# Triangular inverse in one bank: each square made, copied and turned whole, in place of two halves in two banks

## The chip, the cores and the metric

One core of one Trainium2 chip. The time is the device time of the program in microseconds (us); lower is better.

## The reference

One transformer block: four token mixers side by side (gated linear attention, RWKV, Mamba and gated DeltaNet) over 1280 tokens (256 of context, 1024 in a grid), each run forwards and backwards with 4 heads of 64, then a mixture of 64 experts. The change touches two of the mixers. DeltaNet solves, for every chunk of 64 tokens, head and direction, a unit lower triangular system of 64 x 64:

```python
a_kk = jnp.einsum('bnhid,bnhjd->bnhij', kb, k) * jnp.exp(jnp.where(strict, seg, -jnp.inf))
sol = lax.linalg.triangular_solve(a_kk, rhs, left_side=True, lower=True, unit_diagonal=True)
```

RWKV is a step-by-step recurrence there, and the kernel brings it into the same chunked form with the same kind of inverse. In both, a state of 64 x 64 per head and direction then goes from chunk to chunk.

## The kernel before, in words

The program runs in stages, one after the other; every stage has a queue of instructions for each engine, in a written order, tied together by semaphores. `deltanet` (from L1395) and `rwkv` (from L2047) each end in a scan over 10 **pairs** of chunks. One pair holds 8 matrices of 64 x 64 (two directions, two chunks, two heads) for each of two halves of the partitions, so one array of 128 x 512 holds all 16 of a pair. A pair's matrices are inverted while the pair before goes through the state.

`Solve` (L1231) makes the inverse. With N the negated strict part, cut into levels by GpSimd (L1831 to L1833: blocks of 16, the level to 32 and the level to 64), it squares the blocks of 16 three times and sums up Y: square, y2, fourth, y4, eighth, y8; then t32, y32 and t64, y64 join the blocks. For a square TensorE needs both N (copied out of PSUM by ScalarE, L1322) and its transpose M (turned from N by VectorE, L1346; the record of it stands under L1330, the helper). In `scalar` and `vector` these are two operations of 128 x 256 each, for half 0 and half 1; `squared` (L1266) puts half 0 into bank 0 and half 1 into bank 1, and signals after each. The products y2, y4, y8 and the t's and y's go through `product` (L1258), whole, into bank 2 or bank 1; VectorE adds them to Y (L1334), ScalarE copies t32 and t64 (L1325). The eighth isn't turned. `PE_AT`, `ACT_AT` and `DVE_AT` number the signals.

`weave` (L1967) lays out each engine's queue by one list for each mixer; the number is the pair to which an entry belongs, 0 the one being inverted, 1 the next, -1 the one that goes through the state:

```python
DELTA_ORDER = (("square", 0), ("against 0", -1), ("y2", 0), ("solve 0", -1), ("decay 0", -1), ("fourth", 0),
               ("rows", 1), ("result 0", -1), ("y4", 0), ("grams", 1), ("eighth", 0), ("query rows", 1), ("y8", 0),
               ("against 1", -1), ("t32", 0), ("solve 1", -1), ("decay 1", -1), ("y32", 0), ("result 1", -1), ("turn", 1),
               ("t64", 0), ("query grams", 1), ("y64", 0))
```

In DeltaNet "against" is TensorE L1754 and L1762, then VectorE L1915 and L1924 (the right-hand side); "solve" TensorE L1775 and ScalarE L1869; "result" TensorE L1794 and L1802 and VectorE L1936 to L1943 (L1942 where an output is added to an earlier one); "rows" TensorE L1703, VectorE L1887, ScalarE L1859; "grams" TensorE L1717, VectorE L1894, and GpSimd's L1821 and the level masks; "query rows" VectorE L1902, after GpSimd's causal terms (L1821 again); "query grams" TensorE L1729. The first two pairs have no query part. On GpSimd the masks stand ahead of the causal terms. RWKV's list (`WIDE_ORDER`, L1986) weaves in its own grams (TensorE L2329, VectorE L2528), state products and exponentials (ScalarE L2477 to L2479) the same way.

Of the kernel before, what the change touches and what calls it, by code (L numbers as in the profile page):

```python
# [19 lines left out]
NH, HD = 4, 64  # L20
# [82 lines left out]
def each(ap, n):  # L103

    return ap.unsqueeze(1).to_broadcast([ap.shape[0], n, ap.shape[1]])
# [1088 lines left out]
def half(n):  # L1194

    return slice(HD * n, HD * n + HD)
# [34 lines left out]
class Solve:  # L1231

    NPE, NACT, NDVE = 13, 8, 11
    PE_AT = {"square0": 1, "square1": 2, "y2": 3, "fourth0": 4, "fourth1": 5, "y4": 6, "eighth0": 7, "eighth1": 8,
             "y8": 9, "t32": 10, "y32": 11, "t64": 12, "y64": 13}
    ACT_AT = {"square0": 1, "square1": 2, "fourth0": 3, "fourth1": 4, "eighth0": 5, "eighth1": 6, "t32": 7, "t64": 8}
    DVE_AT = {"square0_turned": 1, "square1_turned": 2, "y2": 3, "fourth0_turned": 4, "fourth1_turned": 5, "y4": 6,
              "y8": 7, "y8_turned": 8, "y32": 9, "y32_turned": 10, "y64": 11}  # L1240

    def __init__(self, nc, sem, cr, consts, banks):
        self.nc, self.c, self.banks = nc, consts, banks
# [5 lines left out]
    def pe_done(self, eng, p, what):  # L1249
        eng.wait_ge(self.pe_s, p * self.NPE + self.PE_AT[what])  # L1250

    def act_done(self, eng, p, what):
        eng.wait_ge(self.act_s, p * self.NACT + self.ACT_AT[what])

    def dve_done(self, eng, p, what):
        eng.wait_ge(self.dve_s, p * self.NDVE + self.DVE_AT[what])

# [5 lines left out]
                                             start=True, stop=True)  # L1263
        last.then_inc(self.pe_s, 1)

    def squared(self, n, lhsT, rhs):  # L1266
        for x in range(4 * n, 4 * n + 4):
            for a in range(2):
                r = half(a)
                last = self.nc.tensor.matmul(self.banks[n][r, (x - 4 * n) * HD:(x - 4 * n + 1) * HD], lhsT[r, x],  # L1270
                                             rhs[r, x], start=True, stop=True)
        last.then_inc(self.pe_s, 1)

    def tensor(self, pe, what, p):
        N0, N32, N64, Y = (b[:, p % 2] for b in (self.N0, self.N32, self.N64, self.Y))
        if what == "square":
            pe.wait_ge(self.turned, p + 1)
            for n in range(2):
                self.squared(n, self.M, N0)
        elif what == "y2":  # L1280
            self.act_done(pe, p, "square1")
            pe.wait_ge(self.begun, p + 1)
            if p >= 1:
                self.dve_done(pe, p - 1, "y64")
            self.product(2, self.N, Y)
        elif what == "fourth":
            for n in range(2):
                self.dve_done(pe, p, f"square{n}_turned")
                self.squared(n, self.M, self.N)
        elif what == "y4":  # L1290
            self.act_done(pe, p, "fourth1")
            self.dve_done(pe, p, "y2")
            self.product(2, self.N, Y)
        elif what == "eighth":
            for n in range(2):
                self.dve_done(pe, p, f"fourth{n}_turned")
                self.squared(n, self.M, self.N)
        elif what == "y8":
            self.act_done(pe, p, "eighth1")
            self.dve_done(pe, p, "y4")  # L1300
            self.product(2, self.N, Y)
        elif what == "t32":
            self.dve_done(pe, p, "y8")
            self.product(1, N32, Y)
        elif what == "y32":
            self.act_done(pe, p, "t32")
            self.dve_done(pe, p, "y8_turned")
            self.product(2, self.X, self.T)
        elif what == "t64":
            self.dve_done(pe, p, "y32")  # L1310
            self.product(1, N64, Y)
        elif what == "y64":
            self.act_done(pe, p, "t64")
            self.dve_done(pe, p, "y32_turned")
            self.product(2, self.X, self.T)

    def scalar(self, act, what, p):
        b = [bank[:, :].rearrange("p (x j) -> p x j", x=8) for bank in self.banks]
        if what in ("square", "fourth", "eighth"):
            for n in range(2):  # L1320
                self.pe_done(act, p, f"{what}{n}")
                self.nc.scalar.copy(self.N[:, 4 * n:4 * n + 4], b[n][:, 0:4]).then_inc(self.act_s, 1)  # L1322
        elif what in ("t32", "t64"):
            self.pe_done(act, p, what)
            self.nc.scalar.copy(self.T, b[1]).then_inc(self.act_s, 1)  # L1325

    def vector(self, dve, what, p):
        Y = self.Y[:, p % 2]
        flat = lambda b: b.rearrange("p x j -> p (x j)")
        turn = lambda dst, src: self.nc.vector.transpose(flat(dst), flat(src))  # L1330

        def add(made):
            self.pe_done(dve, p, made)
            self.nc.vector.tensor_tensor(Y, Y, self.banks[2].rearrange("p (x j) -> p x j", x=8),  # L1334
                                         ALU.add).then_inc(self.dve_s, 1)

        if what == "turn":
            turn(self.M, self.N0[:, p % 2]).then_inc(self.turned, 1)
            dve.wait_ge(self.turned, p + 1)
            self.nc.vector.tensor_tensor(Y, self.M, each(self.c.ident, 8), ALU.add).then_inc(self.begun, 1)  # L1340
        elif what in ("square", "fourth"):
            if what == "square":
                dve.wait_ge(self.begun, p + 1)
            for n in range(2):
                self.act_done(dve, p, f"{what}{n}")
                turn(self.M[:, 4 * n:4 * n + 4], self.N[:, 4 * n:4 * n + 4]).then_inc(self.dve_s, 1)  # L1346
        elif what == "y2":
            add("y2")
        elif what == "y4":
            self.dve_done(dve, p, "y2")  # L1350
            add("y4")
        elif what == "y8":
            self.dve_done(dve, p, "y4")
            add("y8")
        elif what == "t32":
            self.dve_done(dve, p, "y8")
            turn(self.X, Y).then_inc(self.dve_s, 1)
        elif what == "y32":
            add("y32")
            self.dve_done(dve, p, "y32")  # L1360
            turn(self.X, Y).then_inc(self.dve_s, 1)
        elif what == "y64":
            add("y64")
# [2299 lines left out]
```

## Time and profile before

| | |
|---|---|
| median of 3 runs | 2801.02 us (2797.8 to 2801.89) |
| the profiled execution | 2796.13 us |
| its span on the core | 2794.5 us |
| TensorE matmul busy | 2504.4 us (90%) |
| VectorE busy | 1538.3 us (55%) |
| ScalarE busy | 974.8 us (35%) |
| GpSimd busy | 838.9 us (30%) |
| L1262, products, 4480 matmul records | 172.8 us |
| granted TensorE clock, mean | 0.952 |

How to read it: the span is one execution as the profiler saw it, and an engine's share of it is an average over stages that have nothing in common. A matmul in 32-bit floats leaves two records; a product or a square of a pair is 16 matmuls, so 32 records. "PE" is TensorE's matmuls, "PEld" its weight loads, DVE is VectorE, ACT ScalarE, POOL GpSimd. "x2" in a row of the order of time means that instructions of one line were merged; the time is then from the first start to the last end. The bracket gives the idle time of the engine before it and who ended it.

### The profile page before, as it was taken

To read this page: it belongs to the slowest core of one execution; us is meant where nothing else is said; L and a number is where in the kernel's file an instruction comes from. 1 tells how busy PE (TensorE), PEld (TensorE's weight loads), DVE (VectorE), ACT (ScalarE), POOL (GpSimd) and SP (SyncE) were. 2 spreads that over 40 slices of the span, in tenths; PEclk is the share of its full clock that TensorE was granted. 3 is DMA by queue.
4 is the path that set the end of the run, shared out by engine and by line. 5 is a ranking of instruction groups with operands and counts; after the bars stand their busy time and mean duration, and the time that the engine had idled before them with its cause. 6 is when DMAs were issued, how large, how long until landed. Compare 5 with 4: busy or idle time off the path is not lost. (4 is left out here: it accounts for less than half of the span.)

```text
span 2794.5 us, 72353 instructions
## 1 busy us (share of the span) xinstructions
PE 2504.4 (90%) x27195; PEld 1379.4 (49%) x27196; DVE 1538.3 (55%) x2685; ACT 974.8 (35%) x1707; POOL 838.9 (30%) x654
## 2 busy tenths in 40 slices
PE   5999899889788869899979797899999999999956
PEld 2448358645578735599834352333333333333322
DVE  3106365844556622476544585566666666666538
ACT  2613115412222202333211113455555555555411
POOL 1000000000244200111100003566666666666565
PEclk9999999899989979999989998999999999999978
DMA  6001402120000020000032207898998899772177
GB/s 243 17 0 47 139 16 91 50 76 1 2 3 4 3 73 1 1 4 5 4 137 95 76 38 309 325 358 348 354 354 319 328 344 357 268 272 89 69 309 315
DMA packets 109099, 408.11 MB, mean 146 GB/s; under 512 B 21001, under 2 KB 37083, under 8 KB 83932
## 3 DMA queue, kind: packets, MB, share of 16 engines
q1 hardware_dynamic: 76636, 287.71, 27.8%
q0 software_dynamic: 20736, 75.51, 6.9%
q10 hardware_dynamic: 11520, 41.95, 3.8%
q8 instruction: 153, 2.51, 0.4%
q14 instruction: 54, 0.44, 0.0%
HBM read 346.40 MB, written 58.72 MB: 145 GB/s over the span
## 5 line engine op out<-in xcount | busy, mean ns | idle before, releaser
L3266 PE MATMUL bank<-arena 128*32 x1280 | 567.6, 596 | 10.5 <-SPq L68 8.1
L3268 PE MATMUL bank<-arena 128*32 128x512 f32 x3840 | 568.6, 596 | 0.0
L3227 POOL COPY arena<-arena 128x2048 f32 x240 | 448.7, 1903 | 330.0 <-PE bank L3300 328.5
L3266 PEld LDWEIGHTS bank<-arena 128*32 128x32 f32 x1280 | 134.7, 110 | 358.4 <-issue 349.3
L3297 PE MATMUL bank<-arena 128*32 x640 | 289.9, 596 | 5.5 <-POOL arena L3227 5.5
L3300 PE MATMUL bank<-arena 128*32 128x512 f32 x1920 | 290.9, 596 | 0.0
L3421 DVE COPY arena<-arena 128x2048 f32 x80 | 139.3, 1741 | 201.6 <-PE bank L3268 183.2
L3358 ACT COPY arena<-arena 128x2048 f32 x80 | 152.0, 1900 | 197.2 <-PE bank L3268 137.8
L1262 PE MATMUL bank<-arena 64*64 64x64 f32 x4480 | 172.8, 226 | 41.9 <-DVE arena L1334 35.1
L3217 POOL DMA_INDIRECT arena<-normed_rows,arena x80 | 165.1, 2064 | 148.8 <-DVE arena L3405 136.9
L1262 PEld LDWEIGHTS bank<-arena 64*64 64x64 f32 x4480 | 157.9, 141 | 47.0 <-DVE arena L1334 37.1
L3297 PEld LDWEIGHTS bank<-arena 128*32 128x32 f32 x640 | 70.4, 110 | 198.4 <-issue 197.9
L3364 ACT COPY arena<-arena 128x2048 f32 x80 | 152.1, 1901 | 0.0
L3268 PEld LDWEIGHTS bank<-arena 128*32 128x32 f32 x3840 | 150.5, 110 | 0.0
L3399 DVE TENSOR_SCALAR arena<-bank,arena 128x128 f32<-128x128 f32 x320 | 109.3, 403 | 40.5 <-PE bank L3251 40.5
L1500 PE MATMUL bank<-arena 128*128 128x512 f32 (+1 forms) x320 | 129.6, 565 | 0.3 <-PE bank L1500 0.3
L517 PE MATMUL bank<-arena 128*128 128x512 f32 (+1 forms) x320 | 127.3, 552 | 0.0
L2462 POOL TENSOR_TENSOR arena<-arena 128x512 f32<-128x512 f32 x10 | 12.9, 1286 | 368.6 <-DVE arena L2528 255.0
L3333 ACT ACTIVATE arena<-bank,arena 128x128 f32<-128x128 f32 x320 | 121.1, 466 | 3.4 <-PE bank L3251 3.4
L351 POOL MEMSET arena<- 128x256 f32 x2 | 0.6, 312 | 394.4 <-POOLq L442 227.5
L1381 DVE SCALAR_TENSOR_TENSOR arena<-arena 128x945 f32<-128x945 f32 (+2 forms) x96 | 113.8, 1220 | 1.7
L2747 PE MATMUL bank<-arena 128*128 128x512 f32 x256 | 111.9, 595 | 0.0
(555 smaller groups left out, 4566.8 us busy)
## 6 DMA issues: line engine op xcount, KB each, us to landing
arena<-in_exp_w_gate_dram SPq DMA_DIRECT2D x64, 1024.0 KB
arena<-in_exp_w_up_dram SPq DMA_DIRECT2D x64, 1024.0 KB
arena<-in_exp_w_down_dram SPq DMA_DIRECT2D x64, 1024.0 KB, 9.3
expert_rows<-arena ACTq DMA_DIRECT2D x80, 512.0 KB
arena<-in_w_mod_dram SPq DMA_DIRECT2D x32, 512.0 KB, 9.1
arena<-in_x_dram SPq DMA_DIRECT2D x16, 512.0 KB, 6.3
arena<-in_w_mod_dram SPq DMA_DIRECT2D x8, 1024.0 KB, 17.8
arena<-in_w_in_dram SPq DMA_DIRECT2D x12, 384.0 KB, 5.9
```

Source lines behind the costliest of these rows:

```text
L517: last = nc.tensor.matmul(k.ps[p % 4][:, 0:width], k.hT[:, c, t * P:(t + 1) * P], W[g][:, c, ws], start=(c == 0), stop=(c == KC - 1))
L1262: last = self.nc.tensor.matmul(self.banks[bank][r, x * HD:(x + 1) * HD], lhsT[r, x], rhs[r, x], start=True, stop=True)
L1500: last = nc.tensor.matmul(k.ps[p % 4][:, 0:w], W[m // 3 % 2][:, c, (m % 3) * P:(m % 3 + 1) * P], k.hT[:, c, a:a + w], start=(c == 0), stop ...
L3217: nc.gpsimd.indirect_dma_start(out=G[:, b.q], out_offset=None, in_=xn_dram, in_offset=bass.IndirectOffsetOnAxis(ap=ID[:, b.q], axis=0)).th ...
L3227: last = nc.gpsimd.tensor_copy(down_copy(u), down_of(slots[u]))
L3266: nc.tensor.matmul(out(SUB - 1), XTT[:, b.q, c, rows(SUB - 1)], W[:, :, c], start=first, stop=end)
L3268: last = nc.tensor.matmul(out(u), XTT[:, b.q, c, rows(u)], WC[:, u, :, c], start=first, stop=end)
L3297: nc.tensor.matmul(ps[6 + half][rows(SUB - 1), :], HT[:, b.q, f, rows(SUB - 1)], W[:, f, c], start=(f == 0), stop=(f == 1))
L3300: last = nc.tensor.matmul(ps[6 + half][rows(u), :], HT[:, b.q, f, rows(u)], WDC[:, u, f, c], start=(f == 0), stop=(f == 1))
L3358: nc.scalar.copy(copy_of(2, LOW), part_of(slot, LOW)).then_inc(lo_a, 1)
L3364: nc.scalar.copy(copy_of(2, HIGH), part_of(slot, HIGH)).then_inc(hi_a, 1)
L3421: nc.vector.tensor_copy(copy_of(0, LOW), part_of(slots[0], LOW))
```

## The change

All three squares use `product` into bank 0. ScalarE makes one copy of 128 x 512 in place of two of 128 x 256, VectorE one transposition of 128 x 512 in place of two; TensorE waits once, for the whole, where it waited once for each half. The signals are renumbered. `squared` is gone. The order of the stages is the same, and `Solve` serves both mixers.

```diff
--- before.py
+++ after.py
@@ -1232,12 +1232,11 @@
 
 
 
-    NPE, NACT, NDVE = 13, 8, 11
-    PE_AT = {"square0": 1, "square1": 2, "y2": 3, "fourth0": 4, "fourth1": 5, "y4": 6, "eighth0": 7, "eighth1": 8,
-             "y8": 9, "t32": 10, "y32": 11, "t64": 12, "y64": 13}
-    ACT_AT = {"square0": 1, "square1": 2, "fourth0": 3, "fourth1": 4, "eighth0": 5, "eighth1": 6, "t32": 7, "t64": 8}
-    DVE_AT = {"square0_turned": 1, "square1_turned": 2, "y2": 3, "fourth0_turned": 4, "fourth1_turned": 5, "y4": 6,
-              "y8": 7, "y8_turned": 8, "y32": 9, "y32_turned": 10, "y64": 11}
+    NPE, NACT, NDVE = 10, 5, 9
+    PE_AT = {"square": 1, "y2": 2, "fourth": 3, "y4": 4, "eighth": 5, "y8": 6, "t32": 7, "y32": 8, "t64": 9, "y64": 10}
+    ACT_AT = {"square": 1, "fourth": 2, "eighth": 3, "t32": 4, "t64": 5}
+    DVE_AT = {"square_turned": 1, "y2": 2, "fourth_turned": 3, "y4": 4, "y8": 5, "y8_turned": 6, "y32": 7,
+              "y32_turned": 8, "y64": 9}
 
     def __init__(self, nc, sem, cr, consts, banks):
         self.nc, self.c, self.banks = nc, consts, banks
@@ -1263,40 +1262,29 @@
                                              start=True, stop=True)
         last.then_inc(self.pe_s, 1)
 
-    def squared(self, n, lhsT, rhs):
-        for x in range(4 * n, 4 * n + 4):
-            for a in range(2):
-                r = half(a)
-                last = self.nc.tensor.matmul(self.banks[n][r, (x - 4 * n) * HD:(x - 4 * n + 1) * HD], lhsT[r, x],
-                                             rhs[r, x], start=True, stop=True)
-        last.then_inc(self.pe_s, 1)
-
     def tensor(self, pe, what, p):
         N0, N32, N64, Y = (b[:, p % 2] for b in (self.N0, self.N32, self.N64, self.Y))
         if what == "square":
             pe.wait_ge(self.turned, p + 1)
-            for n in range(2):
-                self.squared(n, self.M, N0)
+            self.product(0, self.M, N0)
         elif what == "y2":
-            self.act_done(pe, p, "square1")
+            self.act_done(pe, p, "square")
             pe.wait_ge(self.begun, p + 1)
             if p >= 1:
                 self.dve_done(pe, p - 1, "y64")
             self.product(2, self.N, Y)
         elif what == "fourth":
-            for n in range(2):
-                self.dve_done(pe, p, f"square{n}_turned")
-                self.squared(n, self.M, self.N)
+            self.dve_done(pe, p, "square_turned")
+            self.product(0, self.M, self.N)
         elif what == "y4":
-            self.act_done(pe, p, "fourth1")
+            self.act_done(pe, p, "fourth")
             self.dve_done(pe, p, "y2")
             self.product(2, self.N, Y)
         elif what == "eighth":
-            for n in range(2):
-                self.dve_done(pe, p, f"fourth{n}_turned")
-                self.squared(n, self.M, self.N)
+            self.dve_done(pe, p, "fourth_turned")
+            self.product(0, self.M, self.N)
         elif what == "y8":
-            self.act_done(pe, p, "eighth1")
+            self.act_done(pe, p, "eighth")
             self.dve_done(pe, p, "y4")
             self.product(2, self.N, Y)
         elif what == "t32":
@@ -1317,9 +1305,8 @@
     def scalar(self, act, what, p):
         b = [bank[:, :].rearrange("p (x j) -> p x j", x=8) for bank in self.banks]
         if what in ("square", "fourth", "eighth"):
-            for n in range(2):
-                self.pe_done(act, p, f"{what}{n}")
-                self.nc.scalar.copy(self.N[:, 4 * n:4 * n + 4], b[n][:, 0:4]).then_inc(self.act_s, 1)
+            self.pe_done(act, p, what)
+            self.nc.scalar.copy(self.N, b[0]).then_inc(self.act_s, 1)
         elif what in ("t32", "t64"):
             self.pe_done(act, p, what)
             self.nc.scalar.copy(self.T, b[1]).then_inc(self.act_s, 1)
@@ -1341,9 +1328,8 @@
         elif what in ("square", "fourth"):
             if what == "square":
                 dve.wait_ge(self.begun, p + 1)
-            for n in range(2):
-                self.act_done(dve, p, f"{what}{n}")
-                turn(self.M[:, 4 * n:4 * n + 4], self.N[:, 4 * n:4 * n + 4]).then_inc(self.dve_s, 1)
+            self.act_done(dve, p, what)
+            turn(self.M, self.N).then_inc(self.dve_s, 1)
         elif what == "y2":
             add("y2")
         elif what == "y4":
```

## Rows read from the trace of the kernel before

**Rows 1.** Stretch: length, then busy us (x instructions) of PE, PEld, DVE, ACT, POOL; clock

```profile
736.00:982.00 246.00, 194.90 (x5800) 188.97 (x5795) 147.65 (x287) 55.11 (x120) 93.91 (x180) 0.91 0.01 3
1157.00:1391.00 234.00, 220.70 (x7232) 217.67 (x7232) 148.27 (x256) 76.82 (x201) 39.16 (x30) 0.99 0.02 4
```

**Rows 2.** The waits in DeltaNet's scan: who waited for whom, us, times, longest

```profile
DVE arena L1902 <- POOL arena L1821: 43.0, 8, 5.4
```

**Rows 3.** Order of time, DeltaNet's pair 3: start, us, engine, line, shape, [idle before]

```profile
809.48 1.10 PE L1270 MATMUL bank<-arena 64*64 64x64 f32 x32
...
810.16 0.84 ACT L1322 COPY arena<-bank 128x256 f32<-128x256 f32 x2 [1.75 <-PE bank L1270]
...
810.63 0.84 DVE L1330 STREAM_TRANSPOSE arena<-arena 128x256 f32<-128x256 f32 x2 [0.25 <-ACT arena L1322]
...
811.56 0.42 DVE L1915 TENSOR_TENSOR arena<-bank,arena 128x256 f32<-128x256 f32 x1
...
812.02 0.42 DVE L1924 TENSOR_TENSOR arena<-arena 128x256 f32<-128x256 f32 x1
...
812.59 0.68 PE L1775 MATMUL bank<-arena 64*64 64x64 f32 x16
...
818.03 0.69 DVE L1894 SCALAR_TENSOR_TENSOR arena<-bank,arena 128x512 f32<-128x512 f32 x1 [0.20 <-PE bank L1717]
```

**Rows 4.** Order of time, DeltaNet's pair 9: whole copies and turns

```profile
963.71 0.59 ACT L1325 COPY arena<-bank 128x512 f32<-128x512 f32 x1 [3.25 <-PE bank L1262]
...
964.34 1.15 PE L1262 MATMUL bank<-arena 64*64 64x64 f32 x32
...
966.33 0.71 DVE L1330 STREAM_TRANSPOSE arena<-arena 128x512 f32<-128x512 f32 x1
...
966.97 0.38 DVE L1936 TENSOR_TENSOR arena<-arena,bank 128x256 f32<-128x256 f32 x1
```

**Rows 5.** Order of time, DeltaNet's pairs 1 (first two rows) and 7

```profile
762.20 1.10 PE L1270 MATMUL bank<-arena 64*64 64x64 f32 x32
...
764.12 0.39 DVE L1915 TENSOR_TENSOR arena<-bank,arena 128x256 f32<-128x256 f32 x1
...
912.74 0.69 DVE L1334 TENSOR_TENSOR arena<-arena,bank 128x512 f32<-128x512 f32 x1
```

**Rows 6.** Order of time, pair 3 again: from the fourth to y8

```profile
813.08 1.13 PE L1270 MATMUL bank<-arena 64*64 64x64 f32 x32
...
815.23 0.69 DVE L1887 TENSOR_TENSOR arena<-bank,arena 128x512 f32<-128x512 f32 x1
...
816.11 0.42 DVE L1936 TENSOR_TENSOR arena<-arena,bank 128x256 f32<-128x256 f32 x1 [0.19 <-PE bank L1802]
...
817.14 0.69 DVE L1334 TENSOR_TENSOR arena<-arena,bank 128x512 f32<-128x512 f32 x1 [0.28 <-PE bank L1262]
...
817.74 1.13 PE L1270 MATMUL bank<-arena 64*64 64x64 f32 x32
...
819.61 1.13 PE L1262 MATMUL bank<-arena 64*64 64x64 f32 x32
```

**Rows 7.** Order of time, DeltaNet's pair 0: the eighth and y8

```profile
752.04 1.10 PE L1270 MATMUL bank<-arena 64*64 64x64 f32 x32
...
753.61 1.15 PE L1262 MATMUL bank<-arena 64*64 64x64 f32 x32 [0.47 <-ACT arena L1322]
```

**Rows 8.** Order of time, a pair of RWKV's scan

```profile
1209.35 1.15 PE L1270 MATMUL bank<-arena 64*64 64x64 f32 x32
...
1211.21 1.15 PE L1262 MATMUL bank<-arena 64*64 64x64 f32 x32
...
1215.73 0.69 DVE L2528 TENSOR_TENSOR arena<-bank,arena 128x512 f32<-128x512 f32 x1 [0.68 <-PE bank L2329]
```

**Rows 9.** Order of time: TensorE's first product after the wait, pairs 2 and 3

```profile
801.14 1.97 PE L1262 MATMUL bank<-arena 64*64 64x64 f32 x32 [4.24 <-DVE arena L1334]
...
825.43 1.15 PE L1262 MATMUL bank<-arena 64*64 64x64 f32 x32 [3.76 <-DVE arena L1334]
```

## The prediction

> **What bounds the kernel now.** The lines that change run in two stretches only, so I first took the busy time of each engine in them: DeltaNet's scan, 736 to 982 us, and RWKV's, 1157 to 1391 us [rows 1]. In RWKV's, TensorE is busy for 220.7 of 234 us: it is bound by what TensorE issues. In DeltaNet's it is busy for 194.9 of 246 us, so something in a chain sets the pace there. The waits name it: VectorE stands still before line 1902, query rows, 43.0 us over 8 pairs for GpSimd's causal terms (L1821) [rows 2]. GpSimd makes them only behind the three level masks, and those need the negated gram of L1894. So in a DeltaNet pair (ten in 246 us; pair 0 is the first) everything ahead of L1894 counts, and what comes after it and before L1902 has 5 us of cover.
>
> Then I followed one pair, pair 3, in order of time [rows 3]. The square's 32 matmul records start at 809.48 and end at 810.58. ScalarE copies half 0 from 810.16, while TensorE still makes half 1; VectorE turns the halves from 810.63 to 811.47. Next on VectorE's queue is L1915 at 811.56, which subtracts the state's part from the right-hand side, and TensorE's L1775 (solve 0, 812.59) waits for its result. From L1775 on TensorE has next to no idle time up to L1717, the key grams, and L1894 follows them at 818.03. So what delays L1915 delays the pair.
>
> **What a whole square costs in its place.** The products are the same: 32 records, the same order, 1.10 us. 120 half copies become 60 whole ones, 80 half transpositions 40, and the signals and waits between halves go. Not shown before is the copy of a whole square, but the same copy out of bank 1 is [rows 4]: 0.59 us, TensorE's next product 0.04 us after its end. A whole transposition is there too: 0.71 us, and the next VectorE work starts 0.64 us after its start. From TensorE's end to ScalarE's start I take 0.05 us (half of the records of 809.48, and so half 0, are through at about 810.1, and its copy starts at 810.16), from the end of a copy to VectorE about 0.10 (810.16 + 0.37 to 810.63).
>
> *First square, pairs 3 to 9.* The product ends at 810.58, copy 810.63 to 811.22, turned from 811.32, L1915 at 811.96 in place of 811.56: +0.40 us. The y2 product sits behind the state's matmuls and isn't late. Nothing between L1915 and L1894 gives it back: 7 x 0.40 = 2.8 us.
>
> *First square, pairs 1 and 2.* The state's product is shorter there (no query part), and L1915 already starts at 764.12, with the square ended at 763.30 [rows 5]. By the same steps it comes at 764.68: 2 x 0.56 = 1.1 us.
>
> *Fourth.* Product from 813.08 to 814.21; copy 814.26 to 814.85; turned from 814.95; the next, L1887, at 815.59 in place of 815.23, so 0.36 us more [rows 6]. L1936 had 0.19 us of idle time before it and the y4 sum 0.28: both are used up, and L1894 isn't later. In the pairs whose output is added to an earlier one, the y4 sum (912.74) shows no idle time [rows 5], and 0.36 - 0.19, say 0.15, gets through. Of those, pairs 7 and 8 still have an L1894 behind them: 0.3 us.
>
> *Eighth.* Product 817.74 to 818.87, copy to 819.51, y8 product at 819.55 or a little later against 819.61 now, which stands behind the query grams [rows 6]. Nothing; and its sum waits for L1902 anyhow. If that cover went, it would cost what the next case does.
>
> *Ends of the scans.* Where no other work stands between square and product, the wait shows in full: in DeltaNet's first pair the eighth ends at 753.14 and y8 starts at 753.61 [rows 7]; after, 753.14 + 0.05 + 0.59 + 0.04 = 753.82, so +0.21. There are five such places (first square and eighth of DeltaNet's first pair, the eighth of its last, and the eighths of RWKV's first and last): 1.05 us.
>
> *RWKV's pairs.* TensorE is busy through. The fourth ends at 1210.50 [rows 8]; a whole copy ends at 1211.14; the y4 product (1211.21, weights 0.05 ahead) is late by 0.02 us at most. The first square's copy stands there behind the exponentials on ScalarE's queue, so the whole isn't later. VectorE turns 0.1 to 0.2 us later, and its idle 0.68 us before the second L2528 takes that up. 8 x 0.02 = 0.2 us.
>
> Sum: 2.8 + 1.1 + 0.3 + 1.05 + 0.2 = **+5.5 us**. The profiled execution took 2796.13 us (span 2794.5 and 1.6 around it); with +5.5 it is 2801.6. It was the quickest shown: the median of the three runs is 2801.02, 4.9 above. Against that median I forecast **2806.5 us**. A measurement of this kernel can tell about 0.2%, or 5.6 us, from no change, so the forecast stands on that line.
>
> Bounds of the unseen costs: the 0.40 and 0.56 rest on a copy of 0.59, seen 40 times, and on hand-over times of 0.04 to 0.15. With 0.05 us either way on each of nine pairs the sum moves by 0.5; with the fourths let through in all ten pairs by 0.36 it grows by 3.3; with no first square on the path only 1.5 is left.
>
> **TensorE's clock.** After the wait before L1902, TensorE comes back at either level: after 4.24 us idle, in pair 2, the next product took 1.97 us, the 1.2 GHz level; after 3.76 us idle, in pair 3, it took 1.15, the 2.4 GHz level [rows 9]. So 0.82 us hangs on where in that idle time a fall lands. In the profile that product is quick in the six pairs from 3 to 8. Pairs that grow by 0.4 us meet the falls elsewhere. I put it at nothing against the median, whose runs differ by 4.1 us; against the profile up to 6 x 0.82 = 4.9 more, or, where a pair escapes a slow product that it pays now, 0.82 less each, some 2 in all. The Trainium skill (TensorE: Matmul & The Clock Gate, "The HAM clock gate") says that the idle state is the throttled one and that activity releases it, so it would have products after every such pause slow. The row at 825.43 disagrees; by the rule alone that product would be slow in every pair, before and after alike, and the change would get nothing from the clock.
>
> **Rivals.** *A, slower by clearly more:* the drift against the clock's falls puts the product after the wait (t32, L1304) at the low level in five of those six pairs too. It decides once a fall reaches back over that product's start. 5.5 + 5 x 0.82 = 9.6 us: 2810.6. For it: pair 2 shows it. Against: the runs of before sample such positions too.
>
> *B, not slower:* the halves' overlap buys nothing, because L1915 isn't what TensorE really waits for before L1775, or because one long operation hands over quicker than two. The place is the gap of 0.25 us before L1775's weights; it decides if that gap belongs to TensorE's own issue, as its row says. Then only the 1.05, the 0.2 and some of the 0.3 are left: +1.5, or 2802.5. Against: L1775 starts 0.15 us after L1924's end in pair after pair, and L1924 cannot start before L1915 ends.
>
> *C, faster:* two copies of 0.37 are 0.15 us more than one of 0.59, and two half turns take 0.84 us from end to end against 0.71. If ScalarE's or VectorE's occupancy were what each square waits for, 60 x 0.15 would be 9 us less: 2792. Against: ScalarE is idle 1.75 us before the copy [rows 3]. The Trainium skill (VectorE: DVE Perf Modes, "The TRN2 errata", on a fixed extra latency per instruction) argues for this case: fewer and larger operations pay it once. The rows agree on the size; they disagree that it is on the path.
>
> *D, no effect:* the schedule is hidden behind GpSimd altogether, so the time is 2801. That needs L1902's wait to start from something other than L1894.
>
> **How the numbers follow.** Forecast (4 to 7 us) 0.50, split evenly about the line of 5.6 us; A 0.22; B and D together 0.22; C 0.06. Slower by over 0.2%: 0.25 + 0.22 = 0.47. Within 0.2%: 0.25 + 0.22 = 0.47. Faster: 0.06. The range reaches from B to a little over A, 2801.5 to 2811.5, and leaves out D, C, and the worst of the clock.
>
> **What would show it.** Right: in DeltaNet's pairs 3 to 9 the square's matmuls end, one ScalarE copy of 0.59 starts 0.05 us later, and L1915 starts 1.38 us after that end, where it was 0.98; L1775 keeps its 0.15 behind L1924; VectorE's wait before query rows stays at 43 us in all; DeltaNet's scan grows from 246 to some 251 us, and RWKV's by no more than 1. Wrong: L1915 as near to the square as before, DeltaNet's scan as long as before, or a gap on TensorE ahead of y4 in RWKV's pairs. Then the handing over between the engines was misread.

## The result, and the profile after: slower by 9 us, where 5.5 were forecast

Over 12 runs of each kernel the changed one takes 2808.85 us and the one before 2799.81 (medians); the ratio is 1.0032, with a 95% interval of 1.0021 to 1.0044, or +9.0 us (5.9 to 12.3). The forecast was +5.5 and 2806.5 us, with a range of 2801.5 to 2811.5. The sign and the range held, and the size was low. The profiled execution took 2806.82 us with a span of 2805.1.

L1262 is now L1261 (all products, the squares too); the copy of a square is L1309, of t32 and t64 L1312, the turn L1317, the sums L1321. The scans' own lines are 14 lower (L1915 is L1901, L1924 is L1910, L1775 is L1761, L1894 is L1880, L1902 is L1888). One reading of the prediction is put right here, since the text below uses it: L1915 (now L1901) only multiplies the state's product by its decay factors; the subtraction is L1924 (now L1910), right behind it. The chain is the same. The two scans answer to [rows 1]: DeltaNet's from ScalarE's first activation in it (L1841) to VectorE's first output work behind it, then the same 234 us of RWKV's.

```profile
735.50:986.70 251.20, 196.44 (x5824) 191.00 (x5824) 141.57 (x268) 51.24 (x90) 94.72 (x182) 0.91 0.01 3
...
1157.00:1391.00 234.00, 220.24 (x6995) 214.78 (x6995) 138.79 (x229) 72.37 (x168) 39.51 (x30) 0.97 0.02 4
```

VectorE and ScalarE are busy for less, as rival C wanted, and the scan is longer all the same. Measured in every trace from the start of one line to the start of another (DeltaNet: L1855 to L2033 of before; RWKV: the first L2514 to the first L2655), DeltaNet's scan went from 246.67 to 251.13 us (+4.46; forecast +4.9) and RWKV's from 241.11 to 244.67 (+3.56; forecast +0.6). The other 2.6 us of the two spans' 10.6 lie outside the scans, in code that did not change.

The waits in DeltaNet's scan, who waited for whom, us, times, longest; this answers to [rows 2]:

```profile
DVE arena L1888 <- POOL arena L1807: 43.0, 8, 5.4
```

Unchanged to the tenth: everything that L1894 (now L1880) loses, the pair loses. Pair 3 in order of time, against [rows 3] and [rows 6]:

```profile
812.19 2.03 PE L1261 MATMUL bank<-arena 64*64 64x64 f32 x64
...
814.27 0.58 ACT L1309 COPY arena<-bank 128x512 f32<-128x512 f32 x1 [2.21 <-PE bank L1261]
...
814.96 0.71 DVE L1317 STREAM_TRANSPOSE arena<-arena 128x512 f32<-128x512 f32 x1 [0.93 <-ACT arena L1309]
...
815.59 0.39 DVE L1901 TENSOR_TENSOR arena<-bank,arena 128x256 f32<-128x256 f32 x1
816.01 0.43 DVE L1910 TENSOR_TENSOR arena<-arena 128x256 f32<-128x256 f32 x1
...
816.59 0.68 PE L1761 MATMUL bank<-arena 64*64 64x64 f32 x16 [0.50 <-DVE arena L1910]
...
821.14 0.69 DVE L1321 TENSOR_TENSOR arena<-arena,bank 128x512 f32<-128x512 f32 x1 [0.26 <-PE bank L1261]
...
822.03 0.69 DVE L1880 SCALAR_TENSOR_TENSOR arena<-bank,arena 128x512 f32<-128x512 f32 x1 [0.20 <-PE bank L1703]
```

The first row holds an earlier product and the square together; they end at 812.19 + 2.03 = 814.22. The copy starts 0.05 later and takes 0.58, and L1901 starts at 815.59, 1.37 us after the square's end, where 1.38 was forecast and 0.98 measured before. L1761 starts 0.15 after L1910's end, and now shows 0.50 us of idle time. The y4 sum has kept 0.26 us of its idle time, so the whole fourth passes nothing on.

The distances between successive L1894s, each ending in the pair named (us), show where DeltaNet's 4.46 came from; "rest" is from the last of them to the end of the scan:

| ends in pair | 0 | 1 | 2 | 3 | 4 | 5 | 6 | 7 | 8 | rest |
|---|---|---|---|---|---|---|---|---|---|---|
| before | 13.32 | 17.78 | 23.64 | 24.30 | 24.07 | 23.70 | 23.75 | 23.82 | 23.85 | 44.51 |
| after | 15.04 | 18.55 | 24.30 | 24.65 | 24.11 | 24.05 | 24.12 | 24.16 | 24.17 | 44.03 |
| forecast change | 0.21 | 0.77 | 0.56 | 0.40 | 0.40 | 0.40 | 0.40 | 0.55 | 0.55 | 0.61 |
| measured change | 1.72 | 0.77 | 0.66 | 0.35 | 0.04 | 0.35 | 0.37 | 0.34 | 0.32 | -0.48 |

Pairs 1 to 3 and 5 to 8 are near the forecast. **Pair 0** is the mis-sized one: 1.5 us too little was allowed. Its start after the change, and behind it the same stretch before:

```profile
744.76 1.98 PE L1261 MATMUL bank<-arena 64*64 64x64 f32 x32 [7.12 <-DVE arena L1317]
...
746.78 0.58 ACT L1309 COPY arena<-bank 128x512 f32<-128x512 f32 x1 [7.40 <-PE bank L1261]
...
747.42 3.68 PE L1261 MATMUL bank<-arena 64*64 64x64 f32 x64 [0.69 <-ACT arena L1309]
...
750.89 1.66 PE L1689 MATMUL bank<-arena 64*64 64x64 f32 x32
```

```profile
744.27 1.97 PE L1270 MATMUL bank<-arena 64*64 64x64 f32 x32 [7.12 <-DVE arena L1330]
...
746.71 1.76 PE L1262 MATMUL bank<-arena 64*64 64x64 f32 x32 [0.47 <-ACT arena L1322]
...
748.30 1.10 PE L1270 MATMUL bank<-arena 64*64 64x64 f32 x32
...
749.24 1.10 PE L1703 MATMUL bank<-arena 64*64 64x64 f32 x32
```

The idle time before y2 grew by 0.22 us, as the forecast said of such places. But before, TensorE was back at 2.4 GHz within y2 (1.76 us) and made the fourth in 1.10; after, y2 and the fourth both run at 1.2 GHz (3.68 us for the two, 1.0 more than before), and the rise comes within the key rows behind them (L1689, 1.66 us for 1.10). That is 0.2 + 1.0 + 0.6 us, and pair 0 grew by 1.72. The same 11.5 us of each trace, after and then before; the granted clock is the third number from the end (0.55 and 0.70):

```profile
741.00:752.50 11.50, 7.06 (x132) 6.87 (x134) 3.66 (x5) 1.17 (x2) 7.68 (x15) 0.55 0.01 1
```

```profile
741.00:752.50 11.50, 7.76 (x208) 7.58 (x210) 5.59 (x10) 2.12 (x5) 7.20 (x15) 0.70 0.01 3
```

### The profile page after: what moved, and what is told of

Its sections match the earlier page's. It is cut to its first block and busy times, and to the rows that moved or that the text cites. A ratio compares the mean times of both kernels' runs of the same rounds, so it can differ in the third digit from the quotient of the medians.

```text
span 2805.1 us, 72253 instructions
## 1 busy us (share of the span) xinstructions
PE 2511.4 (90%) x27195; PEld 1387.2 (49%) x27196; DVE 1526.8 (54%) x2645; ACT 965.6 (34%) x1647; POOL 838.4 (30%) x654
## 5 line engine op out<-in xcount | busy, mean ns | idle before, releaser
L1261 PE MATMUL bank<-arena 64*64 64x64 f32 x6400 | 241.6, 226 | 52.6 <-DVE arena L1321 34.9
L1261 PEld LDWEIGHTS bank<-arena 64*64 64x64 f32 x6400 | 222.0, 142 | 58.5 <-DVE arena L1321 37.0
L1807 POOL TENSOR_TENSOR arena<-arena 128x128 f32<-128x128 f32 x72 | 27.8, 415 | 283.5 <-SPq L1677 283.5
```

Source lines behind the costliest of these rows:

```text
L1261: last = self.nc.tensor.matmul(self.banks[bank][r, x * HD:(x + 1) * HD], lhsT[r, x], rhs[r, x], start=True, stop=True)
```

## Experiments

Differences in us are the ratio times the median of before in the same group of runs; they can be off the difference of the two medians by a few tenths to 3 us. The first group, e1 to e4, has a median of 2795.80 us for before.

The first group asks whether the loss is DeltaNet's or RWKV's, and the first square's or the others'. An argument names the powers that are made whole; the rest stay halves:

```
-    inv = Solve(nc, sem, cr, H, k.ps[0:3])
+    inv = Solve(nc, sem, cr, H, k.ps[0:3], whole)
e1: whole = all three in DeltaNet, none in RWKV
e2: whole = none in DeltaNet, all three in RWKV
e3: whole = ("square",) in both
e4: whole = ("fourth", "eighth") in both
```

**e1.** 

> Whole squares in DeltaNet's scan, halves in RWKV's. Theory (the chain from the first square over VectorE's turn and L1915 to solve 0): DeltaNet's scan, from ScalarE's L1855 to VectorE's L2033, grows from 246.7 us to about 251 us as in the changed kernel (251.1), RWKV's stays as before; the whole kernel 4 to 5 us slower. Rival (RWKV's scan carries the rest of the 9 us): then this kernel shows only half of the loss, and the next one the other half. Rival (clock): DeltaNet's scan is off from 251 by more than 1 us, and RWKV's first two pairs (28.6 us before, 32.1 after) differ although their code is that of before.

Measured: 2805.49 us against 2795.80, ratio 1.0037 (1.0024 to 1.0050), +10.3 us. DeltaNet's scan 253.46 us, RWKV's 241.09. So nearly all of the loss is DeltaNet's, but it is twice the 4 to 5 us expected; the last distance is 26.48 in place of some 24.1, to which e9 comes back. RWKV's first two pairs take 28.46 us here, with halves.

**e2.** 

> Whole squares in RWKV's scan, halves in DeltaNet's. Theory: DeltaNet's scan 246.7 us; RWKV's pairs 2 to 9 as long as before, its first two pairs at most 0.5 us longer at the same clock; the whole kernel 0 to 1 us slower. Rival (RWKV's scan loses 3.5 us by the change itself): its first two pairs take 32 us here too, with TensorE at its full clock, and the kernel is 3 to 5 us slower. Rival (clock): the first two pairs are longer only where their matmuls run at the low clock.

Measured: 2800.33 us, ratio 1.0014 (1.0000 to 1.0028), +3.9 us (0 to 7.8), where 0 to 1 was expected; the interval holds both. DeltaNet's scan 246.90, RWKV's 242.52, its first two pairs 29.03 us where the changed kernel's profile has 32.10. So those 3.5 us of the changed kernel's profile do not come with whole squares. Whole squares in RWKV cost some tenths to 1.4 us in the traces.

**e3.** 

> Only the first square of each pair whole, the fourth and the eighth in halves, in both mixers. Theory: VectorE's L1915 comes 0.40 us later in DeltaNet's pairs 3 to 9 and 0.56 in pairs 1 and 2; the scan takes 250.5 to 251 us, nearly all of the loss. Rival (the loss is spread over the three squares, some 0.15 each): 248 us.

Measured: 2804.20 us, ratio 1.0023 (1.0013 to 1.0033), +6.4 us (3.6 to 9.2); DeltaNet's scan 250.95, its distances 15.06, 18.33, 24.40, 24.66, 24.16, 24.08, 24.03, 24.10, 24.18. Within 0.25 us these are the changed kernel's own: the first square carries the whole loss that DeltaNet's trace shows.

**e4.** 

> The fourth and the eighth whole, the first square in halves, in both mixers. Theory: DeltaNet's scan grows by 0.4 (eighths of pairs 0 and 9) plus 0.3 (fourths of pairs 7 and 8): 247.4 us; L1915 as before; the kernel within 0.1% of before. Rival (loss spread over the squares): 249.5 us and some 3 to 5 us slower.

Measured: 2795.42 us, ratio 1.0008 (0.9998 to 1.0018); DeltaNet's scan 247.52, first distance 13.24, then 23.56 to 23.82 from pair 3 to 7 and 24.53 in pair 8. In pair 2 it is 25.44, with a VectorE operation of 2.82 us in it (e9). Fourth and eighth are hidden, as the forecast said. That the scan is near the expected 247.4 is luck: the long operation adds some 2 us, and pair 3 and the rest (43.69) are shorter than before by 1.6. In pair 8 the extra 0.7 us are a product of 1.29 for 1.10 and a stop of TensorE amid the 16 matmuls of L1824 (L1802 of before), for which no row names a cause.

The second group, e5 to e8, has a median of 2801.14 us for before. It asks whether it is really L1915's lateness, and what whole squares cost where GpSimd is no longer waited for.

**e5.** An idle VectorE product of 128x448 ahead of L1915, with halves, for the same delay from another cause:

```
+                if u == 0:
+                    TT(JUNK, C[:, 2, 0:448], C[:, 3, 0:448], ALU.mult)
                 dve.wait_ge(ks, s + 1)
                 chain(scaled(t1, four(b_ks[:, 0:GW]), CA, s))
```

> The kernel before, with one idle VectorE multiplication (128 x 448, result unused) ahead of L1915 in each DeltaNet pair, so that L1915 comes some 0.4 us later as with whole squares, by another cause. Theory (only the place of L1915 counts): DeltaNet's gaps between the L1894 grow from 23.8 to 24.1 to 24.2 us, the scan to 250 to 251 us, and t32's start moves against the falls of TensorE's clock by about 0.3 us per pair as in the changed kernel, with the same cost in the timed runs, +0.2 to 0.35%. Rival (whole squares cost something of their own, in signals or in PSUM): the scan grows by clearly less than 3.5 us.

Measured: 2804.22 us, ratio 1.0012 (0.9999 to 1.0026). Distances from pair 4 on 24.06 to 24.39, as with whole squares, but the first is 13.49: a late L1915 accounts for the steady part, not for pair 0. So the scan is 248.97 us, some 2 over before, and misses the expected 250 to 251; pair 0 is 1.5 of what is missing, and pair 2 takes 23.41 us at a granted clock of 0.93, for 24.30 in the changed kernel. RWKV's first two pairs take 31.78 us here, and 31.79 in e7, with halves.

**e6.** Whole squares, with the state's part subtracted (L1915, L1924) ahead of the first square's turn on VectorE's queue:

```
+            order = list(DELTA_ORDER)
+            order[0], order[1] = order[1], order[0]
-            weave(PAIRS, DELTA_ORDER, inverse,
+            weave(PAIRS, order, inverse,
```

> Whole squares, and in VectorE's queue of DeltaNet the right-hand side (against 0: L1915, L1924) ahead of the first square's turn. Theory: L1915 starts at the end of the state's product again, the turn comes after it and the fourth 0.15 us later than before in pairs 3 to 9; the gaps between the L1894 come down to about 24.0, the scan to 248 to 249 us, and the kernel 1 to 4 us slower than before. Rival (the whole squares cost by something else than the place of L1915): gaps of 24.15 and a scan of 251 us as in the changed kernel.

Measured: 2799.38 us, ratio 1.0002 (0.9985 to 1.0018), DeltaNet's scan 246.20, distances from pair 4 on 23.75 to 23.90, and 15.06 in pair 0. Pair 3 in order of time (L1937 is what was L1915, L1946 the subtraction, L1348 the turn, L1797 solve 0):

```profile
812.16 0.58 ACT L1336 COPY arena<-bank 128x512 f32<-128x512 f32 x1 [2.21 <-PE bank L1270]
...
813.10 0.42 DVE L1937 TENSOR_TENSOR arena<-bank,arena 128x256 f32<-128x256 f32 x1 [1.18 <-PE bank L1784]
813.56 0.42 DVE L1946 TENSOR_TENSOR arena<-arena 128x256 f32<-128x256 f32 x1
813.90 0.70 DVE L1348 STREAM_TRANSPOSE arena<-arena 128x512 f32<-128x512 f32 x1
814.13 0.68 PE L1797 MATMUL bank<-arena 64*64 64x64 f32 x16
```

L1937 now starts 0.94 us after the copy's start, where it was 1.32 after it in the changed kernel (814.27 to 815.59); solve 0 follows without idle time. Taking L1915 out from behind the turn gives the steady part back, and pair 0's 1.7 us stay. The scan is even shorter than the 248 to 249 expected. Part of that is the clock: pair 2 takes 22.82 us at a granted clock of 0.93, and pair 3 23.75 at 0.93, where the profile before has 23.64 and 24.30, both at 0.86.

**e7 and e8.** GpSimd's causal terms ahead of its level masks, so that they don't wait for L1894; e7 with halves, e8 with whole squares:

```
                     inv.pe_done(pool, p - 2, "t64")
+                if p >= FIRST:
+                    if p >= FIRST + 1:
+                        pool.wait_ge(arg3, p - FIRST)
+                    terms(MC3, B, H.causal, p, mc3)
                 pool.wait_ge(n_rdy, p + 1)
...
             def gram_q(p):
-                if p >= FIRST:
-                    if p >= FIRST + 1:
-                        pool.wait_ge(arg3, p - FIRST)
-                    terms(MC3, B, H.causal, p, mc3)
```

> Halves as before; GpSimd makes DeltaNet's causal terms ahead of the level masks, so that VectorE's 5.4 us of waiting before the query rows go, and with them TensorE's idle 3.8 us and the falls of its clock. Theory: a pair takes some 19 to 20 us, the scan 246.7 - 8 x (4 to 5) = 207 to 215 us, and the clock stays high in the later pairs. Rival (another wait takes the place, GpSimd's masks for the next turn above all): the pair stays over 22 us.

> The same early causal terms, with whole squares. Theory: against the run with halves and early terms the scan grows by the chain alone, 0.3 to 0.5 us per pair where L1915 still leads to solve 0, 3 to 5 us in all, with no part from the clock. Rival 1 (without its idle time TensorE is bound by its own issue): the two are within 1 us. Rival 2 (the loss of 9 us has nothing to do with the clock): over 7 us between them.

Measured: e7 2761.33 us, ratio 0.9859 (0.9837 to 0.9880); e8 2765.20, ratio 0.9866 (0.9845 to 0.9887). DeltaNet's scan 206.58 and 212.81 us. The scan in e7, and what is left of the wait before the query rows (L1924 in this kernel; it was for GpSimd, 43.0 us):

```profile
731.80:938.40 206.60, 183.73 (x5824) 176.89 (x5824) 149.92 (x288) 56.07 (x120) 98.10 (x182) 0.98 0.02 4
```

```profile
DVE arena L1924 <- PE bank L1751: 9.0, 8, 1.1
```

TensorE's granted clock is 0.98 over the scan, where it was 0.91 with the long pauses. Distances from pair 3 on are 18.95 to 18.96 in e7 but for the last (19.56), and 19.30 to 19.39 in e8 but for the last (19.51). With no wait for GpSimd and no low clock in these pairs, the whole square still costs 0.35 us a pair: it is the chain's own price. Of the 6.2 us between the two scans 1.6 are pair 0's, and 1.2 lie in the last three products of the scan, which e8 has at 1.2 GHz and e7 at 2.4.

The third group, e9 to e11, has a median of 2797.84 us for before. It sizes the change anew and looks for a best version.

**e9.** The changed kernel once more, as its own program.

> The changed kernel once more, to size its cost anew: whole squares everywhere. Theory 1 (a chain cost of 0.3 to 0.4 us a DeltaNet pair, 1.7 in its first pair, 0.4 in RWKV's first two, small clock losses beside): 5 to 7 us over the kernel before, and where this profile has RWKV's first two pairs at 29 us and not at 32, its span is within 4 to 8 us of the one before. Theory 2 (the change itself costs RWKV's first two pairs 3.5 us by the clock): those two pairs at 32 us again and 9 us over. Theory 3 (the clock's falls reach the products after GpSimd's wait in some executions): 7 to 12 us over, with at least one gap between two of DeltaNet's gram subtractions above 25 us.

Measured: 2809.47 us against 2797.84, ratio 1.0043 (1.0028 to 1.0058), +12.0 us (7.8 to 16.2). RWKV's first two pairs 28.99 us: Theory 2 is out. DeltaNet's scan 257.27, 10.6 over before, with distances 15.08, 18.54, 24.33, 24.65, 24.39, **26.65**, 24.27, **26.77**, 24.71. The four stretches that end in pairs 4 to 7; the two with a granted clock of 0.87 are the long ones:

```profile
822.85:847.24 24.39, 20.08 (x615) 19.65 (x613) 14.24 (x28) 4.93 (x9) 9.80 (x19) 0.93 0.02 3
847.24:873.89 26.65, 20.81 (x616) 20.26 (x612) 16.50 (x27) 4.93 (x9) 9.43 (x19) 0.87 0.02 4
873.89:898.16 24.27, 20.00 (x618) 19.63 (x616) 14.20 (x28) 4.93 (x9) 9.80 (x19) 0.93 0.01 3
898.16:924.93 26.77, 20.40 (x612) 20.00 (x609) 16.91 (x30) 4.93 (x9) 9.43 (x19) 0.87 0.01 3
```

By its numbers this is Theory 3, but its mechanism is not the one written there: VectorE is busy 2.3 to 2.7 us longer too, with the same work, and the product behind the wait took 1.40 and 1.17 us in the two long stretches, not 1.97. In order of time, behind the wait in the second stretch (L1946 is the subtraction of the pair's second chunk, which was L1924, L1869 and L1870 are GpSimd's key and value scalings, L1843 its causal terms):

```profile
854.65 1.40 PE L1270 MATMUL bank<-arena 64*64 64x64 f32 x32 [3.55 <-DVE arena L1352]
...
854.96 2.83 DVE L1946 TENSOR_TENSOR arena<-arena 128x256 f32<-128x256 f32 x1
854.98 0.39 POOL L1870 TENSOR_TENSOR arena<-arena 128x128 f32<-128x128 f32 x1
...
856.05 1.46 POOL L1843 TENSOR_TENSOR arena<-arena 128x128 f32<-128x128 f32 x4
...
857.85 1.12 PE L1797 MATMUL bank<-arena 64*64 64x64 f32 x16 [1.80 <-DVE arena L1946]
```

The same place in the changed kernel's own profile:

```profile
853.85 0.40 POOL L1834 TENSOR_TENSOR arena<-arena 128x128 f32<-128x128 f32 x1
853.86 0.68 DVE L1910 TENSOR_TENSOR arena<-arena 128x256 f32<-128x256 f32 x1
...
854.21 0.59 POOL L1833 TENSOR_TENSOR arena<-arena 128x128 f32<-128x128 f32 x1
...
854.59 1.12 PE L1761 MATMUL bank<-arena 64*64 64x64 f32 x16
```

A subtraction of 128x256 that takes 0.43 us alone (816.01 above) takes 0.68 beside GpSimd, and GpSimd's next piece 0.59 in place of 0.40, as if they took turns. In e9 it looks as if VectorE did not get its turn: the operation ends at 857.79, 0.28 us after GpSimd's last piece (856.05 + 1.46 = 857.51), and TensorE idles for 1.80 us. The Trainium skill (SBUF — State Buffer, "SBUF: two separate sides") says that a VectorE instruction with two SBUF inputs and a GpSimd instruction that reads SBUF share one pair of ports, and that whichever starts first has it for the whole instruction while the other fully blocks. The 0.68 agrees with it; the 2.83 is more than one instruction's length.

In the ten profiles with the causal terms where they were, this operation comes behind the query rows 80 times. It takes 2.8 us in 4 of them: e1 once (the 26.48), e4 once (the 25.44), e9 twice. Each of the four ends 0.28 us after GpSimd's row does. In all four, as in those that took 0.68, VectorE starts within 0.02 us of a start of GpSimd's, so the phase at the start does not tell which way it goes.

**e10 and e11.** e8 and e7 with e6's edit as well.

> GpSimd's causal terms ahead, whole squares, and the state's part subtracted ahead of the first square's turn. Theory 1 (what a whole first square costs is only the lateness of that subtraction): the 0.35 us a pair that whole squares cost with the terms ahead go, so DeltaNet's pairs come at 18.96 us or less and the kernel is within 3 us of the one with halves and the terms ahead, 1.4 to 1.5% under the kernel before. Theory 2 (with GpSimd's wait gone, the turned square itself is now what the fourth and TensorE wait for, and turning it later only moves the wait): pairs at 19.2 us or more, 1.3% under at most.

> GpSimd's causal terms ahead, halves, and the state's part subtracted ahead of the first square's turn. Theory 1 (solve 0 waits for that subtraction): it comes 0.3 to 0.6 us earlier and the pairs at 18.5 to 18.8 us in place of 18.96, 2 to 4 us under the kernel with the terms ahead alone. Theory 2 (the turned square is what TensorE waits for next, or TensorE itself is the bound): pairs at 18.9 us or more, no difference.

Measured: e10 2760.85 us, ratio 0.9872 (0.9855 to 0.9890), scan 209.11; e11 2759.89, ratio 0.9864 (0.9849 to 0.9880), scan 206.00. The scan with whole squares gets back 3.7 of the 6.2 us that it was longer than e7's, with 19.02 to 19.39 from pair 3 on, between the two theories; 1.2 of the 3.7 are the last three products, at 2.4 GHz again. With halves the edit brings 0.6 us of scan and no pair under 18.95 from pair 3 on: Theory 2. In time, e7, e8, e10 and e11 can't be told apart; e7 is the simplest.

**e12.** The kernel before once more, as its own program.

> The kernel before once more (halves everywhere), as a second profile of it and to see what two equal programs measure as. Theory 1 (the profile of before that the forecast was made from was a quick and ordinary execution): DeltaNet's scan 246 to 247 us, RWKV's first two pairs at 29 or at 32 us by chance, no VectorE subtraction of 2.8 us behind the query rows, ratio within 0.998 to 1.002. Theory 2 (executions of before have the same rare stalls as the ones with whole squares): at least one subtraction (0.68 us in the profile of before) takes 2.8 us in DeltaNet's scan, which then takes 249 us or more. Theory 3 (the clock's falls drift in before as well): the product after GpSimd's wait is slow in more than two pairs.

Measured: 2797.02 us against 2796.84, ratio 0.9994 (0.9977 to 1.0012). DeltaNet's scan 247.08, first distance 13.53, from pair 4 on 23.85 to 23.89, no operation of 2.8 us, the product behind the wait slow in pairs 1 and 2 alone: Theory 1. Two programs that do the same come out as equal, with an interval of some 0.2% to either side, as the prediction took it.

## Why the prediction was right, and where it was low

**First squares in pairs 1 to 9: right.** The square's end to L1915 took 1.37 us for 1.38. e3 holds the whole loss, e6 gives the steady part back, e5 makes it by another cause, e8 against e7 shows it with the clock out of the way. The size is 0.32 to 0.37 a pair for 0.40 (pairs 3 and 5 to 8), and 0.77 and 0.66 in pairs 1 and 2, for 0.77 (with the eighth of pair 0) and 0.56. Pair 4's 0.04 says little, since its 24.07 before is 23.85 in e12.

**Fourths in pairs 7 and 8: wrong, and small.** 0.15 each was to get through; those pairs grew by no more than the others.

**"Ends of the scans", pair 0: the term that was mis-sized.** "so +0.21" priced the pause alone. With a whole first square in DeltaNet seven profiles have a first distance of 14.9 to 15.2 us (after, e1, e3, e6, e8, e9, e10); with halves seven have 13.2 to 13.5 (before, e2, e4, e5, e7, e11, e12). The 1.7 us are 0.2 of pause and 1.5 of products at 1.2 GHz. In all seven with halves the clock has risen by the end of the fourth (y2 1.68 to 1.97 us, the fourth 1.10 to 1.13); in all seven with a whole first square y2 and the fourth are slow and the rise falls within the key rows (1.53 to 1.77). The clock was looked at only behind the wait for GpSimd, not at the scan's start, where the row of y2 (1.76 us, between the two levels) stood at the edge of a rise. Since e3 has the long distance and e4 has not, it comes with the first square. That the slightly longer pause before y2 is what delays the rise is not shown: it was not tried by itself.

**The rest of the scan** (pair 9 and what is left of pair 8) was to grow by 0.61 and shrank by 0.48 in the profile. The forecast step is there, and a fall of the clock hides it. Up to the last solve the rest takes 39.25 us before (39.29 in e2, 39.28 in e12) and 39.80 after (39.69 to 39.77 in e1, e3 and e9): +0.55. From there to the end of the last product, before and then after:

```profile
976.46:979.78 3.32, 2.85 (x48) 2.48 (x48) 0.61 (x2) 0.37 (x1) 0.00 (x0) 0.55 0.02 5
```

```profile
982.43:984.73 2.30, 1.83 (x48) 1.55 (x48) 0.61 (x2) 0.37 (x1) 0.00 (x0) 1.00 0.03 7
```

The same 24 matmuls run at 1.2 GHz before (in e2 and e12 too) and at 2.4 GHz after (in e1, e3, e4, e5, e6 and e9 too), which gives 1.0 us back. It is luck of position, and the forecast had no term for it.

**RWKV: right.** Without the profiles in which its first two pairs take 32 us (after, e5, e7), the scan is 241.1 to 242.8 us with halves (before, e1, e11, e12; mean 241.7) and 241.6 to 242.5 with all three whole (e2, e6, e8, e9, e10; mean 242.2): +0.4 for +0.6. The timed runs are less sure of it: e2 has +3.9 us, with an interval from 0 to 7.8. The 32 us come once with whole squares and twice with halves; the granted clock over these pairs is 0.80 in the changed kernel's profile and 0.94 in the one before:

```profile
1165.71:1197.81 32.10, 25.78 (x677) 25.04 (x678) 15.96 (x24) 9.62 (x23) 7.51 (x6) 0.80 0.01 3
```

```profile
1159.75:1188.33 28.58, 22.51 (x671) 21.69 (x673) 15.85 (x27) 10.04 (x27) 7.53 (x6) 0.94 0.01 3
```

**Rival A: its mechanism is there, its price is not.** The slower pairs do drift against the falls of the clock: the product behind the wait takes 1.15 us in pair 3, 1.19 in pair 4, and 1.97 in pair 8:

```profile
853.54 1.19 PE L1261 MATMUL bank<-arena 64*64 64x64 f32 x32 [3.77 <-DVE arena L1321]
...
950.04 1.97 PE L1261 MATMUL bank<-arena 64*64 64x64 f32 x32 [3.77 <-DVE arena L1321]
...
952.69 1.50 PE L1261 MATMUL bank<-arena 64*64 64x64 f32 x32
```

But the next whole product then takes 1.50 where it took 1.92, and the distances 24.05 to 24.17 rise by 0.12 us only. And a slow product behind the wait does not go with longer pairs: e4 has it in pairs 2 to 8 (1.83 to 1.98 us), e12 in none of the pairs from 3 on (1.15 us), and the distances that end in pairs 4 to 7 are 23.71 to 23.82 in e4 and 23.85 to 23.89 in e12. So the 0.82 of [rows 9] was no price to be added. That the time came out near A's 2810.6 is no support for A. **B and D** fall with the distances, which grew, and with e6, which undoes it by moving L1915 and L1924 on VectorE's queue; **C** falls with the busy times (VectorE and ScalarE are busy for less, the scan is longer).

**What stays open.** The traced costs come to 4.5 us in DeltaNet and 0.4 in RWKV, near the forecast; the timed ones of whole squares are 9.0, 10.3 (e1) and 12.0 (e9), and 6.4 with the first square alone (e3). Stalls of 2.8 us fill part of it: the four profiles with a whole first square, the turn ahead of L1915 as in the change and the causal terms in place (after, e1, e3, e9) have scans of 251.1, 253.5, 251.0 and 257.3 us, mean 253.2, against 247.0 for before, e2, e4 and e12: +6.2. Whether whole squares make these stalls more frequent can't be said from 3 in 40 places with them and 1 in 40 with halves, and the unprofiled executions show no places. Of the some 9 us timed, 3 or so have no row in any trace. They don't show outside the scans either: what is left of the span without the two scans is 2304 to 2315 us, 2309.7 in the mean of the seven profiles with a whole first square in DeltaNet and 2308.7 in that of the other seven. The sum had neither the 1.5 us of pair 0 nor the stalls nor what stays unexplained. That the time stayed in the range with them is in part luck: the range had been drawn wide enough to hold rival A, whose price was not paid.

## What to carry to other kernels

Where one engine makes a block, a second copies it and a third turns it, two halves in two banks shorten the chain (here by 0.39 us, with a whole copy of 0.58 and a whole turn of 0.71), and the kernel gains by it if the next engine's queue has something urgent behind the last step; merging saves busy time on engines that were idle anyway. Before pricing such an edit ask what is queued behind the last step, since moving that ahead of whole squares (e6) brought the time back to that of the halves, within 0.2%. And the wait that sets the pair was worth 39 us (e7), four times what this change was about: look at what the engine that is waited for does first, and whether it has to.

## What was not expected of the hardware

- 0.22 us more of pause at the start of a scan went with a later rise of TensorE's clock and 1.5 us more for the same matmuls, in all seven kernels that had it.
- A VectorE subtraction with both inputs in SBUF, beside a row of GpSimd operations of 0.4 us, took 0.68 us in 76 of 80 places and 2.8 in 4, until that row had ended, with starts that agree to 0.02 us.
- RWKV's first two pairs take 28.5 to 29.1 us or 31.8 to 32.1, and nothing between, in kernels that have the same code there (e1 with 28.5, e5 and e7 with 31.8).
